# Partial rotary embedding in a two-model kernel: the swap of halves moves from VectorE to TensorE

## The reference

```
half = ROT_DIM // 2                       # 16
x1 = tf[..., :half]
x2 = tf[..., half:ROT_DIM]
out = concat([x1 * cos - x2 * sin, x2 * cos + x1 * sin, tf[..., ROT_DIM:]])
...
q = apply_partial_rope(proj[:, :, g, 0], positions) * scale
k = apply_partial_rope(proj[:, :, g, 1], positions)
o, lse = dilated_window_attention(q, k, v, window, dilation)
```

## Time and profile before

| | |
|---|---|
| median of 3 runs | 3191.89 us |
| lowest and highest | 3186.34 and 3192.02 us |
| the profiled execution | 3191.89 us, of which its span is 3190.1 us |
| mean granted TensorE clock | 0.968 of full |
| busy: PE, PE weight load, DVE, ACT, POOL | 93%, 78%, 54%, 39%, 11% |
| DMA | 441 MB, mean 138 GB/s |
| the attention layer's units | from 18 to about 285 us of the span |

### The profile page before, as it was taken

One profiled execution on the slowest core, in us unless ns is written; L12 is line 12 of the kernel. 1 busy time (PEld: TensorE's weight loads), 2 busy tenths in 40 slices (PEclk: granted clock), 3 DMA queues, 4 the chain that ended last, 5 costly groups with the idle time before them and its releaser, 6 DMA issues.

```text
span 3190.1 us, 41428 instructions
## 1 busy us (share of the span) xinstructions
PE 2964.5 (93%) x17444; PEld 2490.3 (78%) x17444; DVE 1723.3 (54%) x2618; ACT 1258.3 (39%) x2032; POOL 354.1 (11%) x372
## 2 busy tenths in 40 slices
PE   8998999989999989999975399999999999998898
PEld 7997898879977757888752178887887888787898
DVE  6664554655545545444599854443545444444565
ACT  5443443654444434222344343232324322334443
POOL 0000000000013210000178100000000000143100
PEclk9999999999999999999997699999999999999999
DMA  6545666656655443232446132322323233266354
GB/s 228 185 161 187 227 229 219 194 199 226 215 145 87 75 126 119 92 105 93 140 160 241 40 119 94 104 93 94 118 93 118 94 95 103 69 127 92 110 185 133
DMA packets 344459, 441.34 MB, mean 138 GB/s; under 512 B 9777, under 2 KB 329297, under 8 KB 331985
## 3 DMA queue, kind: packets, MB, share of 16 engines
q1 hardware_dynamic: 339744, 428.66, 40.6%
q0 software_dynamic: 4368, 9.45, 4.5%
q10 hardware_dynamic: 160, 0.59, 0.1%
HBM read 437.61 MB, written 1.05 MB: 138 GB/s over the span
## 4 chain that ended last, share of the span: by engine, by line
PE 79%; DVE 13%; ACT 4%; DMA 2%; issue 1%; POOL 0%; SPq 0%; DVEq 0%; ACTq 0%
PE ps L1074 23%; PE ps L1076 23%; PE ps L1075 23%; DVE CV L1876 5%; DVE lo L1566 2%; DVE lo L1569 1%; PE ps L1095 1%; PE ps L1097 1%; PE ps L1096 1%; PE ps L1246 1%; PE ps L1116 1%; ACT hi L1276 1%; PE ps L1107 1%; PE ps L1234 1%; PE ps L1155 1%
## 5 line engine op out<-in xcount | busy, mean ns | idle before, releaser
L1074 PE MATMUL ps<-XN,hi 128*128 128x256 f32 (+1 forms) x3008 | 1020.8, 339 | 78.5 <-DVE lo L1566 37.4
L1075 PE MATMUL ps<-XN,hi 128*128 128x256 f32 (+1 forms) x3008 | 1004.2, 334 | 0.0
L1076 PE MATMUL ps<-XN,lo 128*128 128x256 f32 (+1 forms) x3008 | 1003.8, 334 | 0.0
L1074 PEld LDWEIGHTS ps<-XN,hi 128*128 128x128 f32 x3008 | 580.1, 193 | 189.9 <-issue 36.1
L1566 DVE TENSOR_TENSOR lo<-raw,hi 128x1024 fp32r<-128x1024 f32 (+1 forms) x313 | 390.0, 1246 | 449.9 <-ACT hi L1276 425.4
L1076 PEld LDWEIGHTS ps<-XN,lo 128*128 128x128 f32 x3008 | 579.7, 193 | 54.3
L1075 PEld LDWEIGHTS ps<-XN,hi 128*128 128x128 f32 x3008 | 580.2, 193 | 51.6
L1276 ACT ACTIVATE hi<-raw 128x1024 fp32r<-128x1024 f32 (+1 forms) x313 | 326.4, 1043 | 501.0 <-PE ps L1076 430.5
L1569 DVE TENSOR_TENSOR lo<-raw,hi 128x1024 fp32r<-128x1024 f32 (+1 forms) x313 | 385.1, 1230 | 0.0
L1076 PE MATMUL ps<-H,lo 128*128 128x512 f32 (+1 forms) x1024 | 371.2, 363 | 0.0
L1074 PE MATMUL ps<-H,hi 128*128 128x512 f32 (+1 forms) x1024 | 371.2, 363 | 0.0
(11 more groups left out here) (228 smaller groups left out, 3535.9 us busy)
## 6 DMA issues: line engine op xcount, KB each, us to landing
raw<-in_mlp_w SPq DMA_DIRECT2D x128, 1024.0 KB, 5.2
raw<-in_mod_w SPq DMA_DIRECT2D x96, 1024.0 KB, 5.0
raw<-in_ffn_w_in SPq DMA_DIRECT2D x44, 1024.0 KB, 5.8
raw<-in_attn_w_in SPq DMA_DIRECT2D x36, 1024.0 KB, 5.6
raw<-in_na_wqkv SPq DMA_DIRECT2D x24, 1024.0 KB, 5.2
raw<-in_ffn_w_out SPq DMA_DIRECT2D x16, 1024.0 KB, 5.1
raw<-in_mlstm_w_in SPq DMA_DIRECT2D x12, 1024.0 KB, 5.4
raw<-in_cv_w SPq DMA_DIRECT2D x12, 1024.0 KB, 5.6
```

Source lines behind the costliest of these rows:

```text
L1074: e.matmul(out, whi, xhi, start=first, stop=False)
L1075: e.matmul(out, whi, xlo, start=False, stop=False)
L1076: i = e.matmul(out, wlo, xhi, start=False, stop=last)
```

## The change

The swap is done by a product. A constant matrix `rot` of 32 x 32, with -1 and +1 in it, stands in the constants in place of `sign` (so a row of them is 31 numbers longer). TensorE multiplies it with the first 32 rows of `QK`, 512 columns in float32, into 32 rows of a PSUM bank, and VectorE multiplies that bank by the sine directly. The shuffle is gone; the sign is in `rot`, and the sine activation has no scale. The rotation step now takes one bank in turn, so the bank numbers of later steps differ within the layer.

```diff
-                        ("mmask", 384), ("sign", 1), ("freq", 1), ("amask", 1152)):
+                        ("mmask", 384), ("rot", 32), ("freq", 1), ("amask", 1152)):
...
+    rot = np.zeros((32, 32))
+    for i in range(16):
+        rot[16 + i, i] = -1.0
+        rot[i, 16 + i] = 1.0
+    put("rot", rot)
...
-                    p.do("dil_rotate", pair, g, which)
+                    p.do("dil_rotate", pair, g, which, *p.bank())
...
+    def dil_rotate(pair, g, which, b, u):
+        w.wait_ge(("qk", pair, g, which, 1), free_of(b, u))
+        e.matmul(m.ps[b][0:32, :], const(m, "rot", 32), m.QK[0:32, pair % 2, g, which, :, :], start=True,
+                 stop=True).then_inc(*acc.says(("acc", b, u)))
...
-        e.activation(m.rope[:, 1, :], m.ang[:, 1, :], ACT.Sin, scale=const(m, "sign", 32)).then_inc(*act.says("rope"))
+        e.activation(m.rope[:, 1, :], m.ang[:, 1, :], ACT.Sin).then_inc(*act.says("rope"))
...
-        w.wait_ge(("qk", pair, g, which, 1), "rope")
-        e.stream_shuffle(rt, dst, SWAPPED).then_inc(*dve.says(("swapped", pair, g, which)))
-        w.wait_ge(("swapped", pair, g, which))
-        e.tensor_tensor(rt, rt, sin, ALU.mult).then_inc(*dve.says(("rotsin", pair, g, which)))
-        e.tensor_tensor(dst, dst, cos, ALU.mult).then_inc(*dve.says(("rotcos", pair, g, which)))
+        w.wait_ge(("acc", b, u), "rope")
+        e.tensor_tensor(rt, m.ps[b][0:32, :].rearrange("p (h t) -> p h t", h=2), sin, ALU.mult).then_inc(
+            *dve.says(("free", b, u)))
+        e.tensor_tensor(dst[0:32, :, :], dst[0:32, :, :], cos, ALU.mult).then_inc(
+            *dve.says(("rotcos", pair, g, which)))
         w.wait_ge(("rotcos", pair, g, which))
-        e.tensor_tensor(dst, dst, rt, ALU.add).then_inc(*dve.says(("rot", pair, g, which)))
+        e.tensor_tensor(dst[0:32, :, :], dst[0:32, :, :], rt, ALU.add).then_inc(*dve.says(("rot", pair, g, which)))
```

More of the change, by code:

```diff
@@ L78, in constants @@
     put("mmask", np.concatenate([mm[:128, :], mm[128:, 128:]], axis=1))
-    put("sign", np.repeat([-1.0, 1.0], 16)[:, None])
+    rot = np.zeros((32, 32))
[3 more added lines that the diff above has]
+    put("rot", rot)
     put("freq", np.array(ROPE_FREQ + ROPE_FREQ, np.float32)[:, None])
@@ L196, in reciprocal @@
     def reciprocal(self, *a, **k):
-        return self
-    def stream_shuffle(self, *a, **k):
         return self
@@ L955 @@
 DIL_SCALE = float(P) ** -0.5
-SWAPPED = list(range(16, 32)) + list(range(16))
 def go_through(p, parts):
@@ L1258, in tensor @@
         "product": product, "product_tok": product_tok, "ones": ones_, "condition": condition, "fold": fold,
-        "dil_scores": dil_scores, "dil_turn": dil_turn, "dil_mix": dil_mix, "ml_gate_product": ml_gate_product,
-        "ml_columns": ml_columns, "ml_weights": ml_weights, "ml_products": ml_products, "ml_cell": ml_cell, "ml_close": ml_close, "na_scores": na_scores,
+        "dil_rotate": dil_rotate, "dil_scores": dil_scores, "dil_turn": dil_turn, "dil_mix": dil_mix,
+        "ml_gate_product": ml_gate_product, "ml_columns": ml_columns, "ml_weights": ml_weights,
+        "ml_products": ml_products, "ml_cell": ml_cell, "ml_close": ml_close, "na_scores": na_scores,
         "na_ctx_scores": na_ctx_scores, "na_turn": na_turn, "na_mix": na_mix, "cv_total": cv_total})
@@ L1660, in vector, with dil_rotate @@
     turns = [0]
-    def dil_rotate(pair, g, which):
-        dst = m.QK[0:32, pair % 2, g, which, :, :]
+    def dil_rotate(pair, g, which, b, u):
+        dst = m.QK[:, pair % 2, g, which, :, :]
         cos = m.rope[:, 0, :].unsqueeze(1).broadcast_to([32, 2, S])
```

## The result

| | before | changed |
|---|---|---|
| median | 3190.98 us (4 runs, 3186.34 to 3192.02) | 3206.45 us (4 runs, 3203.53 to 3211.31) |
| span of the profiled execution | 3190.1 us | 3202.4 us |
| the last pair's first mix starts at | 296.66 us | 308.50 us |
| mean granted TensorE clock | 0.968 | 0.967 |

What follows compares the result with a forecast made beforehand. TensorE was taken as the bound, VectorE costing only where TensorE waits for it. Products +29.3, waits -15.1, layer's start -0.6 sum to +13.6 us on 3191.89: 3205.5 us, range 3197 to 3214 us.

Steps and rivals of the forecast that it cites:

- The cost of a product: On TensorE in the attention layer: each of 24 rotation products costs 1.22 us, +29.3 us in all.
- The row for eight 32-column products: Profile row of eight 32-column products on TensorE: 2.04 us, 0.30 of it extra for the smaller column shape.
- the one with the same number of columns: Profile row of two 64-row, 512-column products on TensorE: 1.25 us, 0.38 of it extra; 1.22 was taken nearest to it.
- 1.55: Rival 2, one rotation product on TensorE: both shape extras add up, 1.55 us each, +21.4 us, 3213 us; chance 0.12.
- 0.87: Rival 1, one rotation product on TensorE: no extra for shape, 0.87 us each, +5.6 us, 3197.5 us; chance 0.14.
- The price of the waits: TensorE's three mix waits for VectorE's copy: 4.4, 6.3 and 4.4 us with clock loss, together 15.1 us.
- That they go: The three mix waits vanish, -15.1 us: VectorE's chain ends 1.45 us earlier, TensorE reaches the first 2.44 later, 0.9 spare.
- The layer's start: First two rotations: TensorE waits for ScalarE's tile, yet they cost 1.9 us instead of 2.4, -0.6 us.
- Nothing from VectorE by itself: VectorE's 24 shuffles, 17.3 us busy, count nothing by themselves; the multiplication reading PSUM costs nothing.
- Products beside their neighbours: Rival 4, on TensorE: rotation products run beside full-size ones at 0.255 us each, -9.0 us, 3183 us; chance 0.04.
- Waits that stay: Rival 3, at the mixes: the waits stay or TensorE finds ScalarE late, 3220.6 us; chance 0.08.
- The two on the size of the product: Rivals on one rotation's cost: no shape extra, 3197.5 us, chance 0.14; both extras add up, 3213 us, chance 0.12.

Runs made afterwards that it cites:

- The full-shape kernel: Changed kernel with `rot` padded by zeros to 128 x 128, so the product has all 128 rows and columns; 3201.39 us, ratio 1.0027.
- The kernel with the copy on ScalarE: Kernel before, shuffle kept, with the third PT copy of each head moved from VectorE to ScalarE; 3174.96 us, ratio 0.9945.
- unused: Changed kernel with the shuffle put back; the rotation product runs, its result is only waited for; 3209.95 us, ratio 1.0056.
- the kernel without the shuffle: Kernel before with the shuffle alone taken away, no rotation product, unswapped rows multiplied by the sine; 3182.72 us, ratio 0.9974.
- the other five kernels: Product unused 3209.95 us; shuffle alone taken away 3182.72; copy on ScalarE and no shuffle 3175.58; product in full shape 3201.39; product twice 3225.96.

## Why the prediction held, point by point

- *The cost of a product.* Taken at 1.22 us, measured 1.17 (24 x 1.17 = 28.1 us instead of 29.3). The row for eight 32-column products, with its extra of 0.30, was nearer than the one with the same number of columns. That the product is small in both directions does not add up: 1.55 is out, and so is 0.87; the extra is paid once. The full-shape kernel shows the two terms apart, 0.86 for the columns and 0.31 for the shape. The Trainium skill, "TensorEngine Tiling (Array Packing)", Key Properties, says that a change of tiling mode drains the engine; 0.31 us for there and back, paid once, agree with that, though no run here shows the drain itself.
- *The price of the waits.* 15.1 us, of which 9.0 standing. The kernel with the copy on ScalarE is 16.3 us faster than before by the medians and 14.1 ahead at the last pair's first mix, with 0.97 us of one wait left and about 0.5 gained at the last pair. How much of the price is clock is read from one profiled execution; the last section shows why that part is not to be relied on.
- *That they go.* All three, with 1.1 us to spare at the first where 0.9 were worked out. The product's own length does most of it: unused, it alone brings 2.49 us to 0.23. The prediction counted both contributions and did not say which mattered.
- *The layer's start.* A wait on ScalarE came where it was expected, of 0.47 us instead of the 0.8 worked out. The next unit starts at 40.47 instead of 38.94, and the product ahead of the first rotation at 28.85 instead of 28.78, so two rotations cost 1.5 us there where 1.9 were predicted. That is 0.9 less than their bare 2.3, not the 0.6 of the sum.
- *Nothing from VectorE by itself*, neither the shuffle nor the read of PSUM: the multiplication from PSUM takes 678 ns on average against 680 from SBUF, and the shuffle is worth about 1 us in the kernel with the copy on ScalarE.
- *The sum.* 28.1 - 15.1 - 0.9 = 12.1 us; the mix in the table is 11.8 later. The forecast of 13.6 was too large by the product's 1.2 and the start's 0.3. The prediction left the last pair's wait alone; its length is unchanged, but the clock kept behind it gave 1.4 us that no term has. The medians' 15.5 includes 3 us that no row explains. The forecast lies between the span's difference and the medians', and its start, 3191.89, was 0.9 above the later median; that the time came out within 1 us of it is in part luck.
- *The rivals.* Products beside their neighbours: every one of them paid its full length. Waits that stay: none. The two on the size of the product are settled above.

## What to carry to other kernels

Here, work that was taken off VectorE and given to the bound engine cost its full length there, less only what that engine used to stand; and what it stood could be had without it. 28 us were spent to fill 15 that moving one copy to another engine gives back for nothing. Look what a wait ends on, and move that first. Price the wait with the clock behind it, but count the clock's part as uncertain. The one small matmul tried here among full-size ones was cheaper when it was padded to their shape.

## What was not expected of the hardware

- A shorter wait of TensorE gave back more than its own length. The second wait of the kernel before, 3.59 us, had the granted clock at 0.50, 1.2 GHz, behind it, and a mix of 4.21 us. In the kernel without the shuffle the same wait is 2.28 us, the mix behind it takes 2.23 us and the clock stays at 1.00, 2.4 GHz: 1.3 us off the wait, and 6.3 - 2.4 = 3.9 us off its price (2.4 is the wait with the 0.12 us ahead of it). Two stretches of TensorE in that kernel, around the wait (us, busy, clock, DMA):

```profile
164.00:168.00 4.00, 1.72 (x12) 1.00 0.70 226
168.00:172.00 4.00, 4.00 (x34) 1.00 0.12 37
```

- But a wait's length does not settle what the clock does behind it. The last pair's wait is the same, 3.23 or 2.77 us, with and without the change, behind the same kind of work. In the kernel before and in the one with the copy on ScalarE (282.57, above) the clock falls to 0.50 behind it; in the changed kernel and in the changed one with the copy on ScalarE, the third line here, it stays at 1.00:

```profile
296.66 3.65 PE L1155 MATMUL ps<-PT,V 128*128 128x256 f32 x12 [3.23 <-DVE PT L1701]
308.50 2.23 PE L1160 MATMUL ps<-PT,V 128*128 128x256 f32 x12 [3.23 <-DVE PT L1706]
308.63 2.20 PE L1160 MATMUL ps<-PT,V 128*128 128x256 f32 x12 [2.77 <-ACT PT L1351]
```

  In the other five kernels it falls. The last pair's two mixes lie 6.7 us apart where the clock stays and 8.1 to 9.4 where it falls. What decides is open. So the 3.9 us above are what these traces show of one wait, and not a rule for waits of that length.

- A lone float32 product of 32 x 32 x 512 costs 1.17 us between products of full shape, one of 128 x 128 x 512 costs 0.86.
